# Orders in three mixers of a two-block transformer kernel: where sums of squares, weight splits and turns stand in their engines' queues

## The reference, cut to what matters

```python
def first_block(x, ...):                  # two mixers, each with an FFN behind it
    x = x + short_conv_pool_mixer(h, ...)          # mixer 0
    x = x + swiglu(...)
    x = x + sparse_attn_conformer_mixer(h, ...)    # mixer 1
    x = x + swiglu(...)
def multiscale_pool(v, pool_w, pool_scale):        # inside mixer 0, windows 2, 4, 8, 16
    ...
    means.append((c - prev) / cnt)
    pooled = jnp.stack(means, axis=2) - vg
def second_block(x, ...):                 # block 2
    proj = hn @ w_in                      # queries, keys, values, gates of three attentions
    qa = rms_norm_2(qa.reshape(b, s, H_A, 64), g[0])     # and likewise ka, qb, kb, qc, kc
    ...                                   # MoBA, dilated and sliding-window attention
    merged = jnp.sum(gates * br, axis=2)
    return x + merged @ w_out
```

## Time and profile before

| what | value |
| --- | --- |
| median of 3 runs | 935.57 us |
| the runs | 933.26, 935.57, 937.48 us |
| profiled execution, its own time | 935.31 us |
| its span from first to last instruction | 933.4 us |
| granted TensorE clock over the span | 0.998 of full speed |
| PE busy | 914.7 us, 98% |
| DVE, ACT, POOL busy | 608.3, 485.7, 215.2 us |
| DMA queue of the weights | 55.5% of 16 engines |

### The profile page before, as it was taken

How to read it: one execution, slowest core, us unless ns; L and a number is a source line. 1 busy time by engine, 2 the same in 40 slices (tenths; PEclk the granted TensorE clock), 3 DMA queues, 4 the chain that set the end, 5 groups by cost and what they waited for, 6 DMA issues and landing times.

```text
span 933.4 us, 17115 instructions
## 1 busy us (share of the span) xinstructions
PE 914.7 (98%) x7053; PEld 842.3 (90%) x7053; DVE 608.3 (65%) x827; ACT 485.7 (52%) x729; POOL 215.2 (23%) x177
## 2 busy tenths in 40 slices
PE   9999999999999999999999999999899999999998
PEld 8999999999999798899999997788788888899997
DVE  5876554554589999764545557746574756867664
ACT  6346434434465476744444346465556565547452
POOL 0005990000024230000000001316462704930100
PEclk9999999999999999999999999999999999999999
DMA  8765865666654522465656574546355635563461
GB/s 272 225 227 161 282 204 187 205 194 212 204 185 149 176 97 91 136 225 187 218 180 211 194 228 165 182 147 202 123 176 183 195 115 181 183 208 109 131 231 45
DMA packets 119636, 168.73 MB, mean 181 GB/s; under 512 B 5557, under 2 KB 88597, under 8 KB 119573
## 3 DMA queue, kind: packets, MB, share of 16 engines
q1 hardware_dynamic: 119140, 167.66, 55.5%
q10 hardware_dynamic: 432, 0.19, 0.1%
HBM read 165.38 MB, written 2.46 MB: 180 GB/s over the span
## 4 chain that ended last, share of the span: by engine, by line
PE 74%; DVE 14%; POOL 4%; ACT 3%; DMA 2%; issue 2%; SPq 0%; ACTq 0%; DVEq 0%; POOLq 0%
PE ps L480 21%; PE ps L482 21%; PE ps L481 21%; DVE wlo_sb L445 4%; POOL b_inv_sb L2477 3%; PE ps L922 2%; DMA raw_sb<-w_in_even 2%; PE ps L908 2%; PE ps L935 2%; DVE scratch_sb L1522 2%; ACT whi_sb L422 1%; POOL scratch_sb L2485 1%; PE ps L568 1%; DVE b_ss_sb L2319 1%; PE ps L2097 1%
## 5 line engine op out<-in xcount | busy, mean ns | idle before, releaser
L445 DVE TENSOR_TENSOR wlo_sb<-raw_sb,whi_sb 128x2048 fp32r<-128x2048 f32 x143 | 332.1, 2324 | 182.8 <-ACT whi_sb L422 182.7
L422 ACT ACTIVATE whi_sb<-raw_sb 128x2048 fp32r<-128x2048 f32 x143 | 273.6, 1914 | 161.8 <-PE ps L482 144.7
L480 PE MATMUL ps<-hhi_sb,whi_sb 128*128 128x256 f32 x992 | 274.1, 276 | 2.2 <-DVE wlo_sb L445 1.8
L481 PE MATMUL ps<-hlo_sb,whi_sb 128*128 128x256 f32 x992 | 272.8, 275 | 0.0
L482 PE MATMUL ps<-hhi_sb,wlo_sb 128*128 128x256 f32 x992 | 272.8, 275 | 0.0
L480 PEld LDWEIGHTS ps<-hhi_sb,whi_sb 128*128 128x128 f32 x992 | 190.4, 192 | 4.1 <-DVE wlo_sb L445 2.3
L481 PEld LDWEIGHTS ps<-hlo_sb,whi_sb 128*128 128x128 f32 x992 | 190.4, 192 | 0.5
L482 PEld LDWEIGHTS ps<-hhi_sb,wlo_sb 128*128 128x128 f32 x992 | 190.5, 192 | 0.0
L480 PE MATMUL ps<-whi_sb,hhi_sb 128*128 128x512 f32 (+2 forms) x304 | 115.7, 381 | 0.9 <-DVE wlo_sb L445 0.5
L482 PE MATMUL ps<-whi_sb,hlo_sb 128*128 128x512 f32 (+2 forms) x304 | 112.8, 371 | 0.0
L481 PE MATMUL ps<-wlo_sb,hhi_sb 128*128 128x512 f32 (+2 forms) x304 | 112.6, 370 | 0.0
(11 more groups left out here) (335 smaller groups left out, 1340.8 us busy)
## 6 DMA issues: line engine op xcount, KB each, us to landing
raw_sb<-w_in SPq DMA_DIRECT2D x45, 1024.0 KB, 5.2
raw_sb<-ffn_gate SPq DMA_DIRECT2D x22, 1024.0 KB, 5.3
raw_sb<-ffn_up SPq DMA_DIRECT2D x22, 1024.0 KB, 5.3
raw_sb<-ffn_down SPq DMA_DIRECT2D x22, 1024.0 KB, 4.9
raw_sb<-w_in_even SPq DMA_DIRECT2D x8, 1024.0 KB, 8.4
raw_sb<-w_in_odd SPq DMA_DIRECT2D x8, 1024.0 KB, 5.2
raw_sb<-w_branch SPq DMA_DIRECT2D x6, 1024.0 KB, 5.2
scratch_sb<-bias_rows_dram SPq DMA_DIRECT2D x40, 128.0 KB, 3.2
```

The source lines that it names most:

```text
L422: nc.scalar.activation(place(whi, n0), in_raw(n0), ACT.Copy).then_inc(hi_ready, 1)
L445: nc.vector.tensor_tensor(place(wlo, n0), in_raw(n0), place(whi, n0).bitcast(F32), ALU.subtract).then_inc(lo_ready, 1)
L480: nc.tensor.matmul(dst, l_hi, r_hi, start=first, stop=False)
L481: nc.tensor.matmul(dst, l_hi, r_lo, start=False, stop=False)
```

## The change

In mixer 0, `pooling()` keeps the four adds at t = 2; the scalings and subtractions become `pooled()`, called at t = 4 ahead of `gate(0)`. In mixer 1, PE's eight query transposes go between the two token halves of the gate tile; the first pair's turn in step 1 goes behind the first two taps; DVE's half split of step 31 goes behind the last sum of the branches; the splits of OUT1+3 (ACT and DVE) go behind the first quarter of the tail's SiLU. In block 2, the planner puts "sums" right behind its weights entry, ahead of a job: q1, k1, q2, k2, q3, q4 and kv4 move so, and q0, k0 and k3 stay. All ten "sums" make means and powers per token half, and the scalings wait per half. No operation on the tensors is added but those that come from cutting one into two.

```diff
-        LO_STEP = {10: (OUT1, 0), 14: (OUT1, 1), 18: (OUT1 + 1, 0), 31: (OUT1 + 1, 1)}
+        LO_STEP = {10: (OUT1, 0), 14: (OUT1, 1), 18: (OUT1 + 1, 0)}
...
-            pe.wait_ge(u_scaled, 2)
-            for i in range(NT):
-                for c in range(4):
...
+            def turn_queries():
+                pe.wait_ge(u_scaled, 2)
...
                     mm = product(ps[:, 2 + i, 0:WIDE], hhi[:, k, tok], hlo[:, k, tok], streams(hi[:, k, :], 4),
                                  streams(lo[:, k, :], 4), k == 0, k == KC - 1)
+                if i == 0:
+                    turn_queries()
...
-                if m in TURN_STEP:
-                    f = TURN_STEP.index(m)
-                    pair_t(pe, jobs1, 0, 2 * f, 2 * (f % 2))
-                    pair_t(pe, jobs1, 0, 2 * f + 1, 2 * (f % 2))
+                if m in TURN_STEP and m > 1:
+                    turn_pairs(TURN_STEP.index(m))
...
                     conv3(range(CONV3_AT[m // 2], CONV3_AT[m // 2 + 1]))
+                if m == TURN_STEP[0]:
+                    turn_pairs(0)
...
-                if i == 0:
-                    split_hi(act, OUT1 + 3)
+                    if (i, b) == (0, 0):
+                        split_hi(act, OUT1 + 3)
...
             nc.vector.tensor_tensor(oacc[:, 1, :], oacc[:, 1, :], ot[:, 1, :], ALU.add).then_inc(oacc_ready, 1)
+            split_lo_half(dve, OUT1 + 1, 1, 2)
             dve.wait_ge(ln_mm, 1)
...
-                if i == 0:
-                    split_lo(dve, OUT1 + 3)
+                    if (i, b) == (0, 0):
+                        split_lo(dve, OUT1 + 3)
...
-                    if e[0] in ("half", "empty"):
+                    if e[0] in ("half", "empty", "sums"):
                         continue
                     mixed.append(e)
                     if e[0] == "weights":
-
-                        if body[k + 1:] and body[k + 1][0] in ("half", "empty"):
-                            mixed.append(body[k + 1])
+                        for then in body[k + 1:]:
+                            if then[0] == "weights":
+                                break
+                            if then[0] in ("half", "empty", "sums"):
+                                mixed.append(then)
...
-                    dve.wait_ge(b_squared, 2 * nq + 2)
                     for i in range(NT):
+                        dve.wait_ge(b_squared, 2 * nq + i + 1)
                         nc.vector.tensor_reduce(
...
-                    dve.wait_ge(b_summed, 2 * nq + 2)
-                    nc.vector.tensor_scalar(b_ss[:, nq % 2, 1, :, 0:heads], b_ss[:, nq % 2, 0, :, 0:heads], 1.0 / HD,
-                                            EPS, ALU.mult, ALU.add).then_inc(b_mean, 1)
+                        dve.wait_ge(b_summed, 2 * nq + i + 1)
+                        nc.vector.tensor_scalar(b_ss[:, nq % 2, 1, i, 0:heads], b_ss[:, nq % 2, 0, i, 0:heads], 1.0 / HD,
+                                                EPS, ALU.mult, ALU.add).then_inc(b_mean, 1)
                 elif e[0] == "scale":
                     _, item, nq = e
-                    dve.wait_ge(b_root, nq + 1)
                     for i in range(NT):
+                        dve.wait_ge(b_root, 2 * nq + i + 1)
...
-                pool.wait_ge(b_mean, nq + 1)
-                nc.gpsimd.tensor_tensor(b_inv[:, nq % 2, :, 0:heads], b_ss[:, nq % 2, 1, :, 0:heads],
-                                        nhalf[:, 0:2 * heads].rearrange("p (i h) -> p i h", i=2),
-                                        ALU.pow).then_inc(b_root, 1)
+                for i in range(NT):
+                    pool.wait_ge(b_mean, 2 * nq + i + 1)
+                    nc.gpsimd.tensor_tensor(b_inv[:, nq % 2, i, 0:heads], b_ss[:, nq % 2, 1, i, 0:heads],
+                                            nhalf[:, 0:heads], ALU.pow).then_inc(b_root, 1)
                 if nq < 2:
                     continue
-                pool.wait_ge(b_root, nq + 1)
                 for i in range(NT):
+                    pool.wait_ge(b_root, 2 * nq + i + 1)
...
+            def pooled():
+
                 dve.wait_ge(pool_step, 4)
                 dve.wait_ge(consts_landed, 16)
...
                 if t == 4:
+                    pooled()
                     gate(0)
```

More of the change, by code:

```diff
@@ L1098, in mix1_pe @@
                 mm.then_inc(tile_used, 1)
-            pe.wait_ge(u_scaled, 2)
-            for i in range(NT):
-                for c in range(4):
[L1102 to L1105, removed]
+            def turn_queries():
+                pe.wait_ge(u_scaled, 2)
+                for i in range(NT):
+                    for c in range(4):
+                        at = (c % 2) * T + i * P
+                        mm = nc.tensor.transpose(ps[:, 4 + c // 2, at:at + P],
+                                                 hb[:, i, 4 + 2 * c:6 + 2 * c, :].rearrange("p e d -> p (e d)"),
+                                                 ident[:, :])
+                mm.then_inc(heads_T, 1)
             def turn_twice():
@@ L1190, in branch_rows, with turn_pairs @@
                     mm.then_inc(tile_used, 1)
+            def turn_pairs(f):
+                pair_t(pe, jobs1, 0, 2 * f, 2 * (f % 2))
+                pair_t(pe, jobs1, 0, 2 * f + 1, 2 * (f % 2))
             for m in STEPS1:
```

## The result

The changed kernel takes 925.80 us (median of 4 runs, 925.49 to 925.90), the kernel before 934.86 (4 runs in the same comparison, 933.26 to 937.48): a ratio of 0.9897, 95% interval 0.9875 to 0.9919, or about 1% less. Forecast were 928.5 us and a range from 925.8 to 933.5. The direction was right, the time stands at the very edge of the range, and the gain of the profiled execution (925.90 us, 9.41 less than the one before) was 2.6 us larger than the sum gave.

The account below looks back on a forecast made before the run. PE, busy 914.7 of 933.4 us, was taken as the bound, with nine waits of 8.75 us as the most to gain. The terms summed to -6.83, so 935.31 - 6.83 = 928.5 us; range 925.8 to 933.5.

Parts of the forecast that it names:

- Mixer 0: PE's wait for the split behind four pooling instructions goes once they move to t = 4: -0.88 us.
- the three places of mixer 1: PE's waits at the first pair's turn (+0.37), the half split (-0.43) and the OUT1+3 tail (-0.77).
- the first pair turn: Mixer 1: taps placed in front wait 0.92 for z's low part, replacing the 0.55 wait: +0.37 us.
- Covers: Mixer 0: splits delayed by 2.5 us are each due a tile later, so PE gets no new wait.
- k1's term: Block 2: with sums ahead of the job, PE's whole wait for POOL's scaling goes: -2.42 us.
- q0 and k0: Block 2: sums stay, only the cut in halves acts, gaining 0.59 and 0.65: -1.24 us, ends -1.66 and -0.3.
- who starts first is finished first: Block 2, POOL's power against DVE's split: the first power ends before the split; the second ends 1.65 after it.
- the split starts some 1.0 late: Block 2: DVE's split gives way to POOL's first power by some 1.0 us; its tile is due two tiles on.
- kv4: Block 2: POOL comes free earlier, so 1.10 of PE's 1.27 us wait for ACT goes; bounds -1.27 and 0.
- Passed on: Rival: new PE waits on ACT and DVE at later places take half the gain: 931.9 us, chance 0.14.
- nothing moves: Rival: block 2's scalings still meet splits and waits stay; only mixer 0's 0.88 is left: 934.8 us, chance 0.11.
- Squares in front of the job: Rival: in seven block 2 slots DVE waits 2.0 us for POOL's squares before the job: 942.5 us, chance 0.09.

Follow-up runs that it names:

- Order alone: The kernel before with only the planner's loop changed, so that the sums stand ahead of the job: 929.89 us, ratio 0.9942.
- Halves alone: The kernel before with only block 2's means, powers and waits made per token half: 927.85 us against 935.11, ratio 0.9922.

## Why the prediction was off

- **Mixer 0 and the three places of mixer 1**: right to 0.02 us each, the new waits at 316 and 362 included. The forecast loss of 0.37 at the first pair turn is real: undoing that part alone gains it back. Covers held: the splits delayed in mixer 0 brought no new wait, and none appeared at the moved query turns.
- **The step that failed is k1's term.** The prediction put it as "The whole wait goes: -2.42", and the sum of brackets as "the most the change can bring". The mechanism was right, the size wasn't: the wait cost 2.42 plus, in the profiled execution, 1.7 us of half clock behind it. Work at half clock counts as busy, so no bracket shows it. The table of the kernel before gave the granted clock as 0.998, and 0.2% of 933 us is 1.9 us; I did not ask in which stretch it was missing. Asked, the five microseconds behind the wait show 0.66. With that term the forecast would have been 926.8. The kernel before seems to lose it in 17 of 29 timed runs (by their mean clock), which makes about 1 us on the mean.
- **q0 and k0** were sized -1.24 and gave -1.66. The steps "who starts first is finished first" and "the split starts some 1.0 late" were wrong: they carried to a power what the earlier trace rows show of a scaling. POOL's and DVE's timelines after the change:

```profile
579.26 1.65 POOL L2490 TENSOR_TENSOR b_inv_sb<-b_ss_sb,nhalf_sb 128x8 f32<-128x8 f32 x1 [14.09 <-DVE b_ss_sb L2336]
...
580.88 2.79 POOL L2490 TENSOR_TENSOR b_inv_sb<-b_ss_sb,nhalf_sb 128x8 f32<-128x8 f32 x1
```

```profile
579.89 2.28 DVE L445 TENSOR_TENSOR wlo_sb<-raw_sb,whi_sb 128x2048 fp32r<-128x2048 f32 x1
582.09 0.69 DVE L2343 TENSOR_TENSOR scratch_sb<-scratch_sb,b_inv_sb 128x512 f32<-128x512 f32 x1
583.71 0.69 DVE L2343 TENSOR_TENSOR scratch_sb<-scratch_sb,b_inv_sb 128x512 f32<-128x512 f32 x1 [0.93 <-POOL b_inv_sb L2490]
```

  The split begins 0.63 after the first power and takes its plain 2.28, and the first power takes its plain 1.65: neither holds up the other. The second power starts inside the split and ends 1.50 after it, at 583.67, where the whole power ended 2.76 after its split. That 1.3, and the one scaling (0.65) done early, make 1.9 us, more than the 0.59 and the 1.07 that were to be won.
- **kv4** gave all of its 1.27, inside the bounds; the 1.10 had been chosen between them. Its reductions wait 0.51 for POOL's squares where they waited 3.91:

```profile
776.01 0.42 DVE L2331 TENSOR_REDUCE b_ss_sb<-scratch_sb 128x4 f32<-128x256 f32 x1 [0.51 <-POOL scratch_sb L2487]
```

- **The rivals.** *Passed on* and *nothing moves* are refuted: no wait that the change left alone grew by more than 0.1 us. (The 934.8 of *nothing moves* has the first pair turn's +0.37 in it; by its own words, mixer 1 at 0, it would be 934.4.) *Squares in front of the job* did not come: DVE's L947 waits 21.5 us for PE in 13 places after the change, against 26.6 in 12, so it is still DVE that waits. For POOL's squares it waits at kv4 alone, the 0.51 above. In *Order alone* it waited for them in three places, 3.5 us in all, and no turn of a head was late for it. The price that the Trainium skill's page "Perfetto Trace Analysis", section "Optimizing Scalar/DVE Operations", set on the cuts (an estimate of 0.6 us) isn't seen in PE's waits: with the cuts alone (*Halves alone*) DVE's busy time grew by 1.9 us, 608.3 to 610.2, and PE's waits fell.
- **The range** stopped at the good ends of the waits less 0.8. With the clock's 1.7 it would have begun near 924.

## What to carry to other kernels

A wait of PE can cost more than its length: a stretch at half speed can follow it, which counts as busy time. Look for the granted clock in the stretch behind each long bracket before calling the brackets the ceiling; a mean clock of 0.998 can be 2 us in a program of 930. Profile a kernel more than once before calling such a stretch fixed: here the same wait had it in some executions and not in others. And a late chain can often be mended by any one of several small edits; try each alone before keeping all, since their gains don't add.

## What the hardware showed that was not expected

- Behind waits of 2.36 to 2.42 us the half clock came in two profiles of five, and 17 of 29 timed runs of the kernel before had the mean clock that goes with it; at 2.96 and more it came in all four cases, and at 1.29 and less in none of the 14 profiles. In the two profiles of the kernel before, the clock fell 1.36 and 0.77 us after PE had gone back to work. What decides it in one execution stayed open: nothing was tried that changes it with the wait held fixed.
- A power that had begun 0.63 us ahead of DVE's split ran through it (1.65), and the split too was not held up (2.28). So did the whole power in *Order alone*: 2.90 from 645.02, with a split of 2.28 from 646.46. A power that begins inside a split hardly gets on until the split's end: 2.79 in place of 1.65, 4.88 in place of 2.90. At 653.20 in the earlier trace rows, a scaling of 128x512 did hold a split up (2.60). The Trainium skill's page "SBUF — State Buffer", section "SBUF: two separate sides", says that whichever of the two starts first has the shared ports for its whole instruction. For the scaling the trace agrees; for the 128x8 power it doesn't, and the measurement decides.
